# Feed-forward of a decoder trunk: gate and up projections in seven block products, up left unscaled by the token norm

## What is computed

```python
def rms_norm(x, g):
    y = x32 * lax.rsqrt(jnp.mean(x32 * x32, axis=-1, keepdims=True) + RMS_EPS)
    return (y * g.astype(jnp.float32)).astype(x.dtype)

def swiglu_ffn(h, w_gate, w_up, w_down):
    return (jax.nn.silu(h @ w_gate) * (h @ w_up)) @ w_down

for i in range(DEPTH):
    ...
    h = h + rms_norm(m, norm_g[i, 1])
    f = swiglu_ffn(rms_norm(h, norm_g[i, 2]), ffn_w_gate[i], ffn_w_up[i], ffn_w_down[i])
    h = h + rms_norm(f, norm_g[i, 3])
```

## Time and profile before

| | us |
|---|---|
| median of three runs (2757.94 to 2757.95) | 2757.95 |
| span of the profiled execution | 2753.8 |
| TensorE busy in that span | 2740.9 |
| VectorE | 1577.9 |
| ScalarE | 1109.0 |
| GpSimd | 776.8 |

### The profile page before, as it was taken

How to read it: one execution, slowest core, us unless ns; L and a number is a source line. 1 busy time by engine, 2 the same in 40 slices (tenths; PEclk the granted TensorE clock), 3 DMA queues, 4 the chain that set the end, 5 groups by cost and what they waited for, 6 DMA issues and landing times. The chain is left out here.

```text
span 2753.8 us, 39762 instructions
## 1 busy us (share of the span) xinstructions
PE 2740.9 (100%) x15352; PEld 2350.3 (85%) x15352; DVE 1577.9 (57%) x2157; ACT 1109.0 (40%) x1797; POOL 776.8 (28%) x550
## 2 busy tenths in 40 slices
PE   9999999999999999999999999999999999999999
PEld 7888889888888889988888888889888888889887
DVE  4464676635668676653655455666635465576733
ACT  5322533425257553342443343533424333443422
POOL 0021444303113454330321221543302022254221
PEclk9999999999999999999999999999999999999999
DMA  5323233333620123333332223233333333233331
GB/s 171 92 85 92 79 105 99 97 104 108 167 64 2 40 85 100 103 101 98 106 87 78 82 84 98 86 101 91 102 98 110 90 87 90 77 107 99 90 105 65
DMA packets 448381, 256.37 MB, mean 93 GB/s; under 512 B 9728, under 2 KB 431984, under 8 KB 448112
## 3 DMA queue, kind: packets, MB, share of 16 engines
q1 hardware_dynamic: 446944, 251.69, 31.5%
q10 hardware_dynamic: 1296, 2.75, 0.3%
HBM read 248.11 MB, written 2.10 MB: 91 GB/s over the span
## 5 line engine op out<-in xcount | busy, mean ns | idle before, releaser
L1953 DVE SCALAR_TENSOR_TENSOR w_lo<-w_raw,w_hi 128x1024 fp32r<-128x1024 f32 x461 | 665.1, 1450 | 683.9 <-ACT w_hi L1445 682.7
L1445 ACT ACTIVATE w_hi<-w_raw 128x1024 fp32r<-128x1024 f32 (+1 forms) x460 | 471.2, 1028 | 640.0 <-PE acc L648 544.0
L646 PE MATMUL acc<-a_hi,w_hi 128*128 128x512 f32 (+1 forms) x1688 | 661.9, 392 | 0.3 <-DVE g_lo L2390 0.3
L648 PE MATMUL acc<-a_hi,w_lo 128*128 128x512 f32 (+1 forms) x1688 | 654.8, 388 | 0.0
L647 PE MATMUL acc<-a_lo,w_hi 128*128 128x512 f32 x1496 | 582.7, 389 | 0.0
L648 PEld LDWEIGHTS acc<-a_hi,w_lo 128*128 128x128 f32 x1688 | 317.0, 188 | 65.7
L646 PEld LDWEIGHTS acc<-a_hi,w_hi 128*128 128x128 f32 x1688 | 317.2, 188 | 64.0 <-DVE g_lo L2390 1.2
L647 PEld LDWEIGHTS acc<-a_lo,w_hi 128*128 128x128 f32 x1496 | 281.2, 188 | 56.3 <-issue 1.0
L648 PE MATMUL acc<-hid_hi,w_lo 128*128 128x512 f32 (+1 forms) x704 | 264.5, 376 | 0.0
L647 PE MATMUL acc<-hid_lo,w_hi 128*128 128x512 f32 (+1 forms) x704 | 264.5, 376 | 0.0
L646 PE MATMUL acc<-hid_hi,w_hi 128*128 128x512 f32 (+1 forms) x704 | 264.5, 376 | 0.0
(11 more groups left out here) (439 smaller groups left out, 5451.5 us busy)
## 6 DMA issues: line engine op xcount, KB each, us to landing
w_raw<-ffn_w_gate SPq DMA_DIRECT2D x88, 512.0 KB, 4.0
w_raw<-ffn_w_up SPq DMA_DIRECT2D x88, 512.0 KB, 3.9
w_raw<-gm_w_in SPq DMA_DIRECT2D x64, 512.0 KB, 4.0
w_raw<-ffn_w_down SPq DMA_DIRECT2D x64, 512.0 KB, 3.6
w_raw<-ret_w_in SPq DMA_DIRECT2D x48, 512.0 KB, 3.8
w_raw<-gm_w_out SPq DMA_DIRECT2D x32, 512.0 KB, 3.6
w_raw<-ffn_w_down SPq DMA_DIRECT2D x32, 384.0 KB, 3.2
w_raw<-nsa_w_in SPq DMA_DIRECT2D x21, 512.0 KB, 4.1
```

What stands on the lines that cost most here:

```text
L646: pe.matmul(o_bank, lhs_hi, rhs_hi, start=start, stop=False)
L648: return pe.matmul(o_bank, lhs_lo, rhs_hi, start=False, stop=stop)
L1445: act.activation(w_hi[:, slot, rows_of, :], w_raw[:, slot, rows_of, :], ACT.Copy).then_inc(hi_done, 1)
L1953: dve.scalar_tensor_tensor(w_lo[:, slot, rows_of, :], w_raw[:, slot, rows_of, :], 1.0, w_hi[:, slot, rows_of, :].bitcast(f32), ALU.mult, A ...
```

## The change

Both gate and up pairs may now be seven-product pairs. Groups 2 to 9 form four pairs of groups; in each the even group has a seven-product gate pair and plain up units, the odd group seven-product pairs for gate and for up. That is 12 such halves in a layer instead of 7. A half now issues its three pure products first and its four products with sums last. The up half works in the four banks of `acc`; the last group's gate units move to `st`.

Up is no longer multiplied by R. VectorE takes the up result out of PSUM and multiplies it by silu(gate) in one instruction (`gated`), or, for a seven-product up pair, joins it and multiplies in SBUF (`gated_pair`); GpSimd's products are gone. The feed-forward's output thus lacks a factor R for each token, which the norm behind it removes, except in its epsilon: `SS` starts from epsilon over R squared in place of zero (a Square on ScalarE, a reciprocal over 128 x 512 on VectorE, `eps_of_tokens`), and that norm's root has no bias.

The gained tokens are copied to `a_full` earlier: four of eight copies directly behind the copy of the sums of squares, the other four behind R. Token differences and their splits come one group earlier.

```diff
-SEVEN_FROM, SEVEN_TO = 3, 10
-SEVENS = SEVEN_TO - SEVEN_FROM
+SEVEN_FROM, SEVEN_TO = 2, 10
+UP_SEVEN = (False, True)
+PAIRS = (SEVEN_TO - SEVEN_FROM) // 2
+PAIR_HALVES = 2 + sum(UP_SEVEN)
+HALVES = PAIRS * PAIR_HALVES
...
+        def groups_of(p):
+
+            hn = p * PAIR_HALVES
+            for x, up in enumerate(UP_SEVEN):
+                yield p * 2 + (SEVEN_FROM + x), up, hn + (x if x == 0 else 1 + UP_SEVEN[0])
...
+                def up_unit(i, j, sums=None):
+                    slot = (L["n_up"] + j) % SLOTS
+                    src = cols((ffn_w_gate if j < 2 else ffn_w_up)[l], 0, D_MODEL, i * (2 * P) + (j % 2) * P)
+                    if sums is None:
+                        load(i * 4 + (L["n_up"] + j), slot, src, DT)
+                        return
+                    sp.wait_ge(s_sum, sums)
+                    sp.dma_start(w_raw[:, slot, :, :], src.rearrange("(k p) m -> p k m", p=P)).then_inc(loaded[slot], 16)
+
+                def after_group(i, up, hg):
+
+                    for j in range(2):
+                        up_unit(i + 1, j, sums_base(L, hg + 1))
+                    for j in range(2, 4):
+                        up_unit(i + 1, j, sums_base(L, hg + 2) if up else None)
...
+                    if isinstance(i, int) and i == SEVEN_TO and j < 2:
+                        bank = st[:, j, :]
+                        pe.wait_ge(acc_free, i * 4 + (o0 - 2))
+                    else:
+                        bank = acc[:, (o0 + j) % BANKS, :]
+                        pe.wait_ge(acc_free, i * 4 + (o0 + j - BANKS + 1 if isinstance(i, int) and i < SEVEN_TO else o0))
...
+                def seven_half(i, j, hn, x0, x1, y0, y1):
+
+                    slot0, slot1 = (n0 + j) % SLOTS, (n0 + j + 1) % SLOTS
+                    pe.wait_ge(lo_done, i * 4 + (n0 + j + 1))
+                    block_product(x1[:, first], w_hi[:, slot0, top, :], w_lo[:, slot0, top, :], a_hi[:, top, first], a_lo[:, top, first]).then_inc(s_used, 1)
+                    block_product(x0[:, first], w_hi[:, slot0, bottom, :], w_lo[:, slot0, bottom, :], a_hi[:, bottom, first], a_lo[:, bottom, first]).then_inc(unit_done, 1)
+                    if isinstance(hn, int) and hn == 0:
+                        pe.wait_ge(s_lo, tokens_base(L) + 4)
+                    pe.wait_ge(lo_done, i * 4 + (n0 + j + 2))
+                    block_product(y0[:, first], w_hi[:, slot1, bottom, :], w_lo[:, slot1, bottom, :], t_hi[:, 3, :, :], t_lo[:, 3, :, :]).then_inc(unit_done, 1)
+                    for r, (k, out_half, t) in enumerate([(0, y1[:, first], 0), (2, y1[:, second], 2), (1, x0[:, second], 1), (3, y0[:, second], None)]):
+                        pe.wait_ge(s_lo, sums_base(L, hn) + (r + 1))
+                        rhs_hi = a_hi[:, bottom, second] if t is None else t_hi[:, t, :, :]
+                        rhs_lo = a_lo[:, bottom, second] if t is None else t_lo[:, t, :, :]
+                        block_product(out_half, s_hi_of[k], s_lo_of[k], rhs_hi, rhs_lo).then_inc(s_used, 1)
+
+                def seven_group(i, up, hg):
+                    if isinstance(hg, int) and hg == 0:
                         pe.wait_ge(r_ready, L["b_mid"] + 1)
                     else:
                         pe.wait_ge(acc_free, i * 4 + (o0 - 2))
...
+                    seven_half(i, 0, hg, st[:, 0, :], st[:, 1, :], tr[:, 0, :], tr[:, 1, :])
+                    if up:
+                        pe.wait_ge(acc_free, i * 4 + o0)
+                        seven_half(i, 2, hg + 1, acc[:, 0, :], acc[:, 1, :], acc[:, 2, :], acc[:, 3, :])
+                    else:
+                        for j in range(2, 4):
+                            plain_unit(i, j)
...
+                        act.activation(r4[:, 2 * hf:2 * hf + 2], r4[:, 2 * hf:2 * hf + 2], ACT.Sqrt, scale=1.0 / D_MODEL).then_inc(root_done, 1)
...
                 act.activation(work[:, 2, summed], st[:, 0, summed], ACT.Copy).then_inc(h_part, 1)
+                if b % 2:
+                    tokens(b, 0)
                 split_unit(n0 + AHEAD + 1)
                 act.wait_ge(stat_rd, 3 * b + 1)
                 act.activation(r4[:, 0:CH], r4[:, 0:CH], ACT.Sqrt, scale=1.0 / D_MODEL, bias=r4[:, 6:7]).then_inc(root_done, 1)
                 if not into_gmlp(b):
                     rows_of_root(b)
+                if b % 2:
+                    act.wait_ge(r_ready, b + 1)
+                    act.activation(SS[:, :], R[:, :], ACT.Square, scale=(P / (RMS_EPS * D_MODEL)) ** 0.5)
+                    tokens(b, 1)
+
+            def tokens(b, side):
+
+                for t in range(side * DT // 2, (side + 1) * DT // 2):
+                    last = act.activation(a_full[:, t, :], h[:, t, :], ACT.Copy, scale=gain[:, gain_of(b), t:t + 1])
+                last.then_inc(tokens_in, 1)
...
+                        if i == SEVEN_FROM - 1 and j == 1:
+                            tokens_high()
+                    if i == SEVEN_FROM - 1:
+                        sums_high(0)
...
+                def seven_group(i, up, hg, last):
+
+                    ahead(n0, i, 4, 0, unit_rows(up))
+                    wait(act, acc_free, i * 4 + o0)
+                    p1_copy(hg, 0, st[:, 1, :])
...
+                    ahead(n0, i, 4, 2, unit_rows(not last))
+                    if up:
+                        sums_high(hg + 1)
+                        p1_copy(hg + 1, 1, acc[:, 1, :])
+                    elif not last:
+                        sums_high(hg + 1)
+                    act.wait_ge(m_step, step_base(L, hg) + 4)
                     act.activation(work[:, 0:2, :], work[:, 0:2, :], ACT.Silu).then_inc(silu_done, 2)
                     ahead(n0, i, 4, 3)
+                    if up and not last:
+                        sums_high(hg + 2)
...
+                def eps_of_tokens():
+
+                    dve.wait_ge(tokens_in, 2 * L["layer"] + 2)
+                    dve.reciprocal(SS[:, :], SS[:, :]).then_inc(ss_sum, 1)
+
+                def gated(i, p):
+
+                    dve.wait_ge(unit_done, i * 4 + (n0 + 3 + p))
+                    dve.wait_ge(silu_done, i * 2 + (q0 + p + 1))
+                    tile_at = 2 * i + p if isinstance(i, int) else bass.ds(i * 2 + p, 1)
+                    dve.tensor_tensor(hid_full[:, tile_at, :], acc[:, (o0 + 2 + p) % BANKS, :], work[:, p, :], ALU.mult).then_inc(acc_free, 1)
...
+                        if j < 2:
+                            if i:
+                                dve.wait_ge(acc_free, i * 4 + (o0 + j - 1))
+                            bank = st[:, j, :] if i == SEVEN_TO else acc[:, (o0 + j) % BANKS, :]
+                            dve.wait_ge(unit_done, i * 4 + (n0 + j + 1))
+                            dve.tensor_tensor(work[:, j, :], bank, R[:, :], ALU.mult).then_inc(acc_free, 1)
+                        else:
+                            gated(i, j - 2)
+                        if i == SEVEN_FROM - 1 and j == 1:
+                            tokens_low()
+                    if i == 0:
+                        eps_of_tokens()
+                    if i == SEVEN_FROM - 1:
+                        sums_low(0)
...
+                def gated_pair(i, hu):
+
+                    dve.wait_ge(m_step, step_base(L, hu) + 4)
+                    dve.wait_ge(silu_done, i * 2 + (q0 + 2))
+                    tiles = slice(2 * i, 2 * i + 2) if isinstance(i, int) else bass.ds(i * 2, 2)
+                    dve.tensor_tensor(hid_full[:, tiles, :], work[:, 2:4, :], work[:, 0:2, :], ALU.mult).then_inc(acc_free, 2)
+
+                def seven_group(i, up, hg, last):
+
+                    ahead(n0, i, 4, 0, unit_rows(up))
                     ahead(n0, i, 4, 1)
-                    ahead(n0, i, 4, 2, unit_rows(i, 2))
-                    join(i)
-                    if not (isinstance(i, int) and i == SEVEN_TO - 1):
-                        sums_low(i + 1)
-                    leave(i * 4 + (n0 + 2), work[:, 2, :], (o0 + 2) % BANKS, R[:, :])
-                    ahead(n0, i, 4, 3)
-                    leave(i * 4 + (n0 + 3), work[:, 3, :], (o0 + 3) % BANKS, R[:, :])
+                    ahead(n0, i, 4, 2, unit_rows(not last))
+                    join_gate(i, hg)
+                    if up:
+                        sums_low(hg + 1)
+                        scale_gate(i)
+                        ahead(n0, i, 4, 3)
+                        join_up(hg + 1)
+                        if not last:
+                            sums_low(hg + 2)
+                        gated_pair(i, hg + 1)
+                    else:
+                        scale_gate(i)
+                        gated(i, 0)
+                        if not last:
+                            sums_low(hg + 1)
+                        ahead(n0, i, 4, 3)
+                        gated(i, 1)
...
-                wait(pool, stat_f, 2 * (b - 1))
-                pool.memset(SS[:, :], 0.0).then_inc(ss_sum, 1)
+                if b % 2:
+                    wait(pool, stat_f, 2 * (b - 1))
```

(45 more changed lines are left out.)

186 lines of the change are left out of this document (71 added, 115 removed).

## The result

The changed kernel takes **2774.34 us** (median of 4 runs, 2773.24 to 2776.22), the one before 2757.94: ratio 1.006, 95% interval 1.0046 to 1.0074. It is slower, and 1.3 us beyond the upper end of my range. The profiled execution took 2774.5 us with a span of 2772.8, 19.0 more than before.

What follows compares the result with a forecast made beforehand. TensorE, busy 2740.9 of a 2753.8 us span, was taken as the bound; waits of +24.8 less 16.0 gained gave +8.8, span 2762.6, time 2766.8 us. Range 2749 to 2773, from the waits' bounds alone 2762 to 2771.

Steps and rivals of the forecast that it cites:

- Part 1: Feed-forward: 20 more seven-product halves in all, 0.80 us gained each, -16.0 us.
- Part 2: Steady-state groups of the feed-forward: sums and splits ready with 2.2 and 1.5 us to spare, no wait, taken as 0.
- rival (E): Waits at transposes and behind R, plus late weight loads in steady state: 12 us more, 2778.8 us; chance 0.07.
- Part 3: Feed-forward entry: VectorE's additions of squares and GpSimd's first token difference take turns; TensorE waits 2.2 us per layer.
- Rival (D): Only the chain behind R makes TensorE wait, additions of squares slip in ahead: 2758.0 us; chance 0.11.
- Part 4: From R to group 2's first sum product: longer chain, TensorE waits 4.0 us per layer (about 0.9, 0.7, 2.4).
- the sum: Whole kernel: 4 x (2.2 + 4.0) = +24.8 us of waits, less 16.0, gives +8.8 us, span 2762.6.
- A: Main case: waits at the transposes and behind R both come, 2766.8 us, own range 2762 to 2771; chance 0.60.

Runs made afterwards that it cites:

- difference held back: Changed kernel, with GpSimd's first token difference waiting until VectorE has read the totals of the squares: 2760.35 us.
- reciprocal later: Changed kernel, with VectorE's reciprocal of SS moved from the end of group 0 to behind the first low weight sums: 2757.79 us.
- all chain edits: Changed kernel, first token difference after VectorE's read of the totals, reciprocal behind the low sums, second four token copies at the end of ScalarE's group 0: 2744.98 us.
- before, difference first: Kernel before, with four early token copies and GpSimd's first token difference ahead of its group 0 products: 2769.59 us.
- all up pairs: Up pairs of all eight groups in seven products, on the 2740.23 us kernel (three moved instructions, low sums earlier): 2778.1 us.

## Why the prediction failed where it did

Against the span of before (2753.8), with the waits by the view of waits, 0.16 us for each new wait (a matmul of 512 columns is recorded 0.39 us long but the next starts 0.23 behind it, so the listed idle time falls short by 0.16), and half the time at half clock (the most that it can cost; stretches in the attention are counted too):

| kernel | halves | new waits | unlisted | clock | sum | measured |
|---|---|---|---|---|---|---|
| after | -16.0 | +22.3 | 16 x 0.16 = 2.6 | +10.2 | +19.1 | +19.0 |
| difference held back | -16.0 | +14.7 | 12 x 0.16 = 1.9 | +3.4 | +4.0 | +4.7 |
| reciprocal later | -16.0 | +13.5 | 8 x 0.16 = 1.3 | +5.1 | +3.9 | +3.3 |
| all chain edits | -16.0 | +3.3 | 4 x 0.16 = 0.6 | +1.7 | -10.4 | -9.3 |
| before, difference first | 0 | +7.7 | 4 x 0.16 = 0.6 | +8.5 | +16.8 | +15.8 |

- **Part 1, right.** 0.80 us a half was forecast, 0.81 measured over 16 halves (0.73 to 0.83, by what it is taken against). The Trainium skill's fixed cost (page "TensorE: Matmul & The Clock Gate", section "Wait — 56ns, not 53.3ns?") would have made it 1.19 us by my estimate; the measurement does not agree.
- **Part 2, right.** No wait in a later group; rival (E) did not come. The run with all up pairs shows how near its edge is.
- **Part 3, right.** 2.2 us forecast, 1.95 + 0.16 = 2.1 measured, and made again in the kernel before by moving one instruction. Rival (D), in which the additions slip in ahead, falls. The Trainium skill, page "SBUF — State Buffer", section "SBUF: two separate sides", says that the pair of ports is locked for a whole instruction; the addition of 2.43 us against 0.42, ending just behind GpSimd's difference of 2.38, agrees.
- **Part 4, right as a whole, wrong inside.** Forecast 4.0 us, measured 1.6 + 0.5 + 2.1 = 4.2 (listed 5.9, 1.3 and 7.8 over four layers, and 0.16 each). Unit 5 was forecast at 0.9 us. VectorE was on time: its low part ended 2432.62 - 2423.53 = 9.1 after R, as forecast. TensorE was earlier than I had it: I read 2408.93 in the earlier trace rows as the last matmul of unit 3, but it is the third of unit 4; eight k tiles from 2401.75, with the transposes between, end at 2408.47. Unit 5 was wanted at 7.4, not 8.1. The last wait came out smaller than forecast, as the earlier ones had already pushed TensorE back. The end of the chain was nearly exact: the first sum product starts 2456.09 - 2423.53 = 32.6 behind R, forecast 32.7. Against the right start (28.74 - 0.69 = 28.05) that is 4.5 us in this layer, so that the 4.0 was short by the misread row. By this the table's unlisted 0.16 is somewhat too little and its clock, an upper bound, somewhat too much; the agreement of 24.9 with 24.8 is in part luck.
- **The failing step is the sum.** "4 x (2.2 + 4.0) = +24.8" priced each wait as the idle time that it is, and that came out at 22.3 + 2.6 = 24.9. It left out the clock: up to 10.2 us lost in stretches at half clock, 8.5 of them behind the new waits, 1.7 in the attention. The forecast span was 2762.6 and the measured one 2772.8, just these 10.2. The range of A, "from the bounds of the waits", could not hold that either. The earlier trace rows were taken from an execution with the clock at 1.000 throughout, and I took that clock for given.
- **A second slip made the miss look smaller.** "The span leaves 4.15 us outside it" set the median of before against the span of one of its fastest executions. In the later runs the time is 1.7 to 2.1 us more than the span of the same execution (2774.5 and 2772.8; 2755.8 and 2753.8). With 2 us in place of 4.15 the forecast would have been some 2764.6, and the miss 9.7 us and not 7.5. By luck the slip stood for something real: other executions of before are slower than the profiled one.

The runs agree with this one by one: the four executions of the changed kernel are 2773.24 us at a mean clock of 0.997, 2774.17 and 2774.5 at 0.996, 2776.22 at 0.995. That fits stretches as the cause of the spread too, and one now and then in before's own runs (2755.8 to 2760.0, clock 1.000 and 0.999). It is not shown: only one execution of each kernel has a trace.

**Open**: which waits are followed by a stretch. Of twenty waits of 1.90 to 1.97 us at the two places (eight in the changed kernel, four each with the difference held back, with the reciprocal moved, and in the kernel before with the difference first) twelve have a half-clock stretch that begins within 2 us of their end: 2 + 3, 1, 3 and 3. The rest have none, and I cannot say what decides it. Length matters: in the twelve profiles none of the 45 waits of 1.0 to 1.7 us has a stretch within 2 us of it, and four of the five of 2.3 to 2.7 us (all up pairs in seven products) have one. Nor can I say what makes the stretch in the attention near 780 us, which comes and goes between profiles with the same code there. A listed wait is not needed for it. With the difference held back TensorE shows no idle time from 764 us on, only many small products, when the clock falls:

```profile
770.00:772.00 2.00, 2.00 (x23) 1.93 (x23) 1.57 (x2) 1.97 (x4) 0.00 (x0) 1.00 0.29 72
772.00:774.00 2.00, 2.00 (x31) 1.94 (x30) 1.73 (x4) 1.95 (x4) 0.38 (x1) 0.86 0.37 92
774.00:776.00 2.00, 2.00 (x6) 1.52 (x6) 1.83 (x3) 1.93 (x5) 0.91 (x1) 0.50 0.44 123
```

## What to carry to other kernels

Price an idle time of TensorE of some 2 us twice: as the wait, and with some six chances in ten (twelve of twenty here) of up to 1.7 us more at half clock behind it; the 45 waits of 1.0 to 1.7 us had none. When a gain does not appear, do not give the change up: the 16 us were in it, and three moved instructions (a difference, a reciprocal, four copies) and one earlier set of low sums brought them out. Before moving work to another engine's free time, look at what shares its port in the same 2 us.

## What the runs showed of the hardware

- Behind waits of 1.9 to 2.0 us TensorE ran 3.4 us at half its clock in twelve of twenty cases; in twelve profiles 45 waits of 1.0 to 1.7 us were followed by none, nor were the 88 waits of at most 0.8 us of one of them. Keeping TensorE busy with unread products kept the clock at 1.00, and the kernel was 6.6 us faster with more work in it.
- In the attention the clock fell for 3.4 us in two profiles (773 and 768 us) with no wait of TensorE listed there.
- A GpSimd instruction of 2.4 us that began 0.2 us ahead of a VectorE addition of 0.42 us held it until its own end: the addition took 2.43 us, the three in a row 4.38 and 4.39 us in two kernels, against 2.37 and 2.38 where GpSimd ran only its own short additions beside them.
- VectorE's reciprocal of 128x512 takes 3.34 us, as the earlier trace rows had it from another stage.
